# A hybrid decoder layer on one core: when the first q tiles and the scans' step sizes are computed

## What is computed

```python
mod = jax.nn.silu(c) @ w_ada[layer] + b_ada[layer]
sh1, sc1, g1, sh2, sc2, g2 = jnp.split(mod[:, None, :], 6, axis=-1)
h = rmsnorm(x, norm1_g[layer]) * (1.0 + sc1) + sh1
proj = h @ w_in[layer]
q, k, v, ga, gb, z, xbc, dt = jnp.split(proj, offsets, axis=-1)
...
ya = diff_attention(q, k, v, positions, ...)   # rmsnorm and rope of q and k, 8 heads, two softmaxes each
yb = ssd_mixer(z, xbc, dt, ...)
# in ssd_mixer:
dtp = jax.nn.softplus(dt.astype(jnp.float32) + dt_bias.astype(jnp.float32))
a_neg = -jnp.exp(a_log.astype(jnp.float32)).reshape(SSD_GROUPS, SSD_HEADS_PER_GROUP)
y = ssd_chunked(xs * dtp[..., None], dtp * a_neg, bm, cm)   # needs cumulative sums of dtp * a_neg
```

## Time and profile before

| | |
|---|---|
| median of 3 runs | 1936.28 us (1935.77 to 1940.3) |
| profiled execution | 1932.19 us, span 1930.4 us |
| PE busy | 1606.1 us (83%) |
| DVE busy | 1322.3 us (68%) |
| ACT busy | 934.2 us (48%) |
| mean granted clock of PE | 0.915 |

### The profile page before, as it was taken

How to read it: one execution, slowest core, us unless ns; L and a number is a source line. 1 busy time by engine, 2 the same in 40 slices (tenths; PEclk the granted TensorE clock), 3 DMA queues, 4 the chain that set the end, 5 groups by cost and what they waited for, 6 DMA issues and landing times.

```text
span 1930.4 us, 22703 instructions
## 1 busy us (share of the span) xinstructions
PE 1606.1 (83%) x7242; PEld 1255.4 (65%) x7243; DVE 1322.3 (68%) x1714; ACT 934.2 (48%) x1136; POOL 306.1 (16%) x298
## 2 busy tenths in 40 slices
PE   6697698699999999998974728999999779999950
PEld 1485586477777777775863516787777558877740
DVE  2486557777674775766556657798888448888849
ACT  2325433532234343342322127788888448888830
POOL 1000000011020101101100271222222122222210
PEclk9798899899999999998986869999999889999985
DMA  8021022068212122120431049899999459999948
GB/s 287 28 87 44 1 87 88 1 234 313 88 63 88 66 66 88 46 86 3 164 116 66 1 149 353 315 378 376 354 370 385 175 194 371 368 364 357 345 171 355
DMA packets 103538, 361.43 MB, mean 187 GB/s; under 512 B 19116, under 2 KB 29552, under 8 KB 76432
## 3 DMA queue, kind: packets, MB, share of 16 engines
q1 hardware_dynamic: 71472, 278.41, 38.9%
q0 software_dynamic: 27040, 62.07, 8.8%
q10 hardware_dynamic: 4928, 19.78, 2.6%
HBM read 352.18 MB, written 43.66 MB: 205 GB/s over the span
## 4 chain that ended last, share of the span: by engine, by line
PE 60%; DMA 15%; DVE 14%; ACT 4%; issue 4%; POOL 2%; ACTq 0%; SPq 0%; POOLq 0%; DVEq 0%
PE psum L1311 16%; PE psum L1313 15%; PE psum L1312 15%; DMA rawm<-in_w_exp_up 8%; DMA modraw<-in_w_ada 2%; PE psum L720 2%; POOL slot_table L571 2%; DMA rawm<-in_w_exp_down 2%; DVE ring L879 2%; PE psum L1533 2%; DVE ofin L962 1%; PE psum L1478 1%; PE psum L1466 1%; DVE modacc L1632 1%; PE psum L1438 1%
## 5 line engine op out<-in xcount | busy, mean ns | idle before, releaser
L879 DVE TENSOR_TENSOR ring<-rawm,ring 128x2048 fp32r<-128x2048 f32 x192 | 436.0, 2286 | 39.8 <-ACT ring L807 39.6
L807 ACT ACTIVATE ring<-rawm 128x2048 fp32r<-128x2048 f32 x192 | 368.1, 1918 | 94.5 <-DMA rawm<-in_w_exp_up 41.0
L1311 PE MATMUL psum<-ring,xT 128*128 128x512 f32 x528 | 223.8, 424 | 27.2 <-DVE ring L879 22.4
L1618 DVE TENSOR_TENSOR hl<-raw,hl 128x2048 fp32r<-128x2048 f32 x59 | 135.4, 2296 | 119.1 <-ACT hl L1104 118.5
L1313 PE MATMUL psum<-ring,xT 128*128 128x512 f32 x528 | 211.1, 400 | 0.0
L1312 PE MATMUL psum<-ring,xT 128*128 128x512 f32 x528 | 210.9, 399 | 0.0
L1311 PE MATMUL psum<-hl,hT 128*128 128x512 f32 x416 | 165.4, 398 | 11.2 <-DVE hT L1919 11.2
L666 POOL DMA_INDIRECT y_rows<-yb,row_of x64 | 98.4, 1538 | 439.7 <-ACT yb L851 430.1
L1313 PE MATMUL psum<-hl,hT 128*128 128x512 f32 x416 | 162.9, 392 | 0.0
L1312 PE MATMUL psum<-hl,hT 128*128 128x512 f32 x416 | 162.9, 392 | 0.0
L1311 PE MATMUL psum<-hT,hl 128*128 128x512 f32 x320 | 136.9, 428 | 1.3 <-DVE hl L1618 1.3
(11 more groups left out here) (374 smaller groups left out, 3078.7 us busy)
## 6 DMA issues: line engine op xcount, KB each, us to landing
rawm<-in_w_exp_gate SPq DMA_DIRECT2D x64, 1024.0 KB, 11.8
rawm<-in_w_exp_up SPq DMA_DIRECT2D x64, 1024.0 KB, 14.7
rawm<-in_w_exp_down SPq DMA_DIRECT2D x64, 1024.0 KB, 9.6
raw<-in_w_in SPq DMA_DIRECT2D x36, 1024.0 KB, 5.1
modraw<-in_w_ada POOLq DMA_DIRECT2D x16, 1024.0 KB, 7.0
ysum<-y_rows ACTq DMA_DIRECT2D x16, 1024.0 KB, 9.1
raw<-in_w_ada SPq DMA_DIRECT2D x8, 1024.0 KB, 9.7
raw<-in_w_branch_b SPq DMA_DIRECT2D x8, 1024.0 KB, 5.1
```

Of the source, the lines that this page charges most:

```text
L807: A(ring[:, slot, 1, :], rawm[slot][:], ACT.Copy).then_inc(S["m_hi2"], 1)
L879: TT(ring[:, slot, 0, :], rawm[slot][:], ring[:, slot, 1, :].bitcast(F32), ALU.subtract).then_inc(S["m_lo2"], 1)
L1311: M(dst, lhs(0), rhs(0), start=first, stop=False)
L1618: TT(hl[:, slot, 0, :], raw[slot][:], hl[:, slot, 1, :].bitcast(F32), ALU.subtract).then_inc(S["lo_done"], 1)
```

## The change

The first two tiles of q are computed inside the step `h`: two blocks behind the transposes, PE issues the three matmuls of one channel block for each of the two tiles, into banks 0 and 1 (`products`). Their own steps then issue nothing on PE (`ahead`). The step sizes become a step kind of their own, `dt`, in three parts that stand in the list behind q's second tile (the dt weights' products, ACT's copy), behind q's fourth tile (transposes, softplus, `aa`), and behind k's third tile (cumulative sums, exponential, last product). They no longer stand in `h`. This holds for the first four heads; for the others (hf = 1) the list is as it was.

```diff
@@ -87,6 +87,7 @@
 
 
 CONV = (4, 5, 0, 1, 2, 3)
+DT_AT = {("q", 1): 0, ("q", 3): 1, ("k", 2): 2}
 
 
 def plan_steps(w):
@@ -151,8 +152,14 @@
     item("h", 0)
     late = iter([(j, h) for j in range(4, 12) for h in range(2)])
     for hf in range(2):
-        whole(base("row", ("q", hf), halves(w["w_in"], OQ + hf * 512), 4))
-        whole(base("row", ("k", hf), halves(w["w_in"], OK + hf * 512), 4))
+        for n, at in (("q", OQ), ("k", OK)):
+            b = base("row", (n, hf), halves(w["w_in"], at + hf * 512), 4)
+            for o in range(4):
+                out(b, o)
+                if (n, hf) == ("q", 0) and o < 2:
+                    steps[-1]["ahead"] = True
+                if hf == 0 and (n, o) in DT_AT:
+                    item("dt", DT_AT[n, o])
         whole(base("row", ("v", hf), halves(w["w_in"], OV + hf * 512), 4))
         item("qkT", hf)
         item("attn", hf)
@@ -1145,14 +1152,16 @@
                     a.wait_ge(S["params"], 16 * 9)
                     a.wait_ge(S["params_act"], 16 * 7)
                     A(wdt_hl[:, :, 0, :], wdt[:], ACT.Copy).then_inc(S["small_hi"], 1)
+                elif kind == "dt" and tag == 0:
                     a.wait_ge(S["smallT_ps"], 1)
                     A(hsplit[0:32, 0, :], psum[0:32, 6, :], ACT.Copy).then_inc(S["smallT_ev"], 1)
-
+                elif kind == "dt" and tag == 1:
                     a.wait_ge(S["dt_dve"], 1)
                     L(A(dwk[:, 2], dwk[:, 1], ACT.Exp))
                     A(dtb[:, 1], dtb[:, 1], ACT.Exp).then_inc(S["dt_exp"], 1)
                     a.wait_ge(S["dt_dve"], 2)
                     A(dwk[:, 4], dwk[:, 3], ACT.Ln).then_inc(S["dt_exp"], 1)
+                elif kind == "dt":
                     a.wait_ge(S["dt_ps"], 2)
                     A(expo[:].rearrange("p a t h -> p (a t h)"), psum[:, 5, 0:384], ACT.Exp).then_inc(S["dt_exp"], 1)
                 elif kind in ("row", "col", "branch"):
@@ -1313,6 +1322,17 @@
                 return M(dst, lhs(1), rhs(0), start=False, stop=last)
 
 
+            def products(s, k):
+
+                u = s["base"]["u"][k // 4]
+                if s["o"] == 0 and k % 4 == 0:
+                    pe.wait_ge(S["lo_done"], u["m"] + 1)
+                wv = lambda q: hl[:, u["n"] % RING, 1 - q, :].rearrange("p (k n) -> p k n", n=512)
+                ins = three(bank(s["o"]), lambda q: hT[:, k, q, s["o"] * P:(s["o"] + 1) * P],
+                            lambda q: wv(q)[:, k % 4, :], k == 0, k == KD - 1)
+                if k == KD - 1:
+                    ins.then_inc(S["proj_done"], 1)
+
             pe.wait_ge(S["params"], 16 * 9)
             pe.wait_ge(S["consts"], 1)
             tr(psum[:, 6, 0:113], pr1[0:113, :], ident[0:113, 0:113]).then_inc(S["par_T"], 1)
@@ -1346,29 +1366,38 @@
                     wait(pe, S["mod_ev"], tag)
                     M(bank(7), ones[:], modacc[:, tag % 2], start=True, stop=True).then_inc(S["mod_ps"], 1)
                 elif kind == "h":
+                    ahead = [q for q in steps if q.get("ahead")]
                     pe.wait_ge(S["xr_ready"], NT)
-                    for k in range(KD):
-                        wait(pe, S["h_tmp"], k - 1)
-                        for t in range(NT):
-                            ins = tr(psum[:, 4 + k % 2, t * P:(t + 1) * P], x_rows[:, t, k * P:(k + 1) * P], ident[:])
-                        ins.then_inc(S["xT_ps"], 1)
-
+                    for k in range(KD + 2):
+                        if k < KD:
+                            wait(pe, S["h_tmp"], k - 1)
+                            for t in range(NT):
+                                ins = tr(psum[:, 4 + k % 2, t * P:(t + 1) * P], x_rows[:, t, k * P:(k + 1) * P], ident[:])
+                            ins.then_inc(S["xT_ps"], 1)
+                        if k >= 2:
+                            pe.wait_ge(S["h_lo"], k - 1)
+                            for q in ahead:
+                                products(q, k - 2)
+                elif kind == "dt" and tag == 0:
                     pe.wait_ge(S["small_lo"], 1)
-                    pe.wait_ge(S["h_lo"], KD)
                     for k in range(KD):
                         ins = three(psum[0:32, 6, :], lambda q: wdt_hl[:, k, q, :], lambda q: hT[:, k, q, :],
                                     k == 0, k == KD - 1)
                     ins.then_inc(S["smallT_ps"], 1)
+                elif kind == "dt" and tag == 1:
                     pe.wait_ge(S["smallT_ev"], 1)
                     for t in range(NT):
                         ins = tr(psum[:, 4, t * 32:(t + 1) * 32], hsplit[0:32, 0, t * P:(t + 1) * P], ident[0:32, 0:32])
                     ins.then_inc(S["dt_ps"], 1)
+                elif kind == "dt":
                     pe.wait_ge(S["dt_dve"], 3)
                     for q, tri in enumerate((upper, later, ones)):
                         for t in range(NT):
                             ins = M(psum[:, 5, (q * NT + t) * 32:(q * NT + t + 1) * 32], tri[:], aa[:, t, :],
                                     start=True, stop=True)
                     ins.then_inc(S["dt_ps"], 1)
+                elif s.get("ahead"):
+                    continue
                 elif kind in ("row", "col", "branch"):
                     name, b, o = tag[0], s["base"], s["o"]
                     nk = len(b["u"]) * b["ks"]
@@ -1737,6 +1767,7 @@
                     L(TT(dt_, dwk[:, 2], dwk[:, 5], ALU.add))
                     L(TT(aa[:], dtp[:], over_h(dtb[:, 1]), ALU.mult))
                     TS(aa[:], aa[:], -1.0, None, ALU.mult).then_inc(S["dt_dve"], 1)
+                elif kind == "dt" and tag == 2:
                     v.wait_ge(S["dt_exp"], 3)
                     L(TT(dtdec[:], dtp[:], expo[:, 1], ALU.mult))
                 elif name in ("q", "k"):
```

## The result

| | before | changed |
|---|---|---|
| median | 1935.38 us (1927.39 to 1940.3, 8 runs) | 1924.85 us (1919.26 to 1928.27, 8 runs) |
| ratio | | 0.9948, 95% interval 0.9926 to 0.997 |
| profiled execution | 1932.19 us, span 1930.4 | 1925.31 us, span 1923.5 |

The change makes the kernel faster, by 0.5% in this comparison. It repeated at 0.9966 (0.9949 to 0.9983) and 0.9961 (0.9945 to 0.9977) with the same code. The forecast was 0.3%, and 1924.85 us lies under its range of 1926 to 1938.

What follows compares the result with a forecast made beforehand. PE was taken to bound the changed stretch, DVE close behind. PE's earlier q tiles, less the 9.5 us wait and 2.3 us of clock, ended v 5.8 us sooner: 1930.5 us from the 1936.28 median, range 1926 to 1938.

Steps and rivals of the forecast that it cites:

- both q tiles done: End of step h: q's first two tiles, computed among the transposes, finish at 73.8 us; bounds 72 and 84.
- clock behind it: PE's k third tile after the idle time: 4.6 us at half rate, a loss of 2.3 us; bounds nothing and 5.4.
- scan matrices: PE's 24 small matmuls after k's third tile: 3.3 us, between 2.6 and 5.1, where they took 5.14 before.
- shift at v's end: PE's turn from v's last tile to q's transposes: 149.5 in place of 155.3, 5.8 us sooner.
- The hold: Second dt part waits for q's norm on DVE and delays ACT's first k eviction; PE idle 9.5 us before k's third tile.
- the variant with -4.4: A 1.38 us drain per table switch would lengthen the wait for k's eviction by 1.4 us, making the sum -4.4.
- The interleaved part: Rival: the eight rounds among the transposes in h run at low clock; +6.6 us, 1942.9 us, chance 0.08.
- Slow and stay slow: Rival: low clock lasts through k's third tile, scan matrices and seven next products; net +0.2, 1936.5 us, chance 0.17.
- a change without the hold: Rival: ACT evicts k before the second dt part, DVE becomes the bound; -17.7, 1918.6 us, chance 0.05.
- The paragraph ahead of the rivals: Took the shift of 5.8 us to 1926.4 against the profiled execution and 1930.5 against the median of 1936.28 us.
- How the numbers follow: Section giving the forecast 0.70; chances faster 0.48, same 0.41, slower 0.11; range of 1926 to 1938 us.
- the bound: What a measurement of this kernel tells from no change: 0.3%, 5.8 us, just the forecast shift.

Runs made afterwards that it cites:

- the filled hold: Against the changed kernel, 40 products without use on PE ahead of k's third tile; 11.8 us under the kernel before, ratio 0.9939.
- the kernel with ACT's share later: Against the changed kernel, only ACT's share of the second dt part moved, behind k's second eviction; 6.9 us under the kernel before, ratio 0.9964.

## Why the prediction was right and wrong

The path was right, nearly to the microsecond. Counted from the first scaled tile, in the profile of the changed kernel:

| step, as predicted | predicted | measured |
|---|---|---|
| both q tiles done | 73.8 - 56.4 = 17.4 us | 75.48 - 57.93 = 17.55 |
| PE idle at k's third tile | 9.5 us | 9.16 from start to start, 9.00 idle |
| clock behind it | 2.3 us | 8.18 - 5.44 = 2.74 |
| scan matrices | 3.3 us | 2.60 |
| shift at v's end | 5.8 us | 99.08 - 92.93 = 6.15; 6.6 on the means of three |
| the whole, by ratio | 5.8 us | 10.0, 6.6 and 7.5 |

The hold was where it was put, with the engines named: ACT waited 17.11 us for `dwk`, PE for ACT. The Trainium skill (TensorE: Matmul & The Clock Gate, "HAM oscillation — how this bites in real kernels") says that a burst of products behind an idle stretch starts cold. The changed kernel's trace agrees, with a mean of 0.66 over the 8.18 us behind the hold, and the filled hold priced that at 2.6 us apart from the wait. The drain beside a table load, which the prediction takes from the Trainium skill (ScalarE: Activation LUTs, "What ACT_TABLE_LOAD costs"), isn't there: the logarithm began 1.29 us after the load (110.41, 111.70), so the variant with -4.4 falls.

Some of the agreement is luck. In `h` the clock rose about 5.5 us after the first scaled tile, where I had 4.4 (60.8 - 56.4): it stood at 0.50 over 60 to 62 and at a mean of 0.64 over 62 to 64. Rounds of 1.83 us, where I had 1.9, made up for most of that. And I read the earlier trace rows wrongly: DVE's split that starts at 153.55 takes 2.29 us and so ends behind v, not 2 us short of its end. It cost nothing, since in the changed kernel the same split ends at 148.2, ahead of the transposes at 150.66.

**Of the rivals.** The interleaved part didn't run at the low clock: 0.84 over the 17.55 us, with the slow part at its start. Slow and stay slow didn't come about either, as the matrices at 1.00 show; the kernel with ACT's share later shows that it does come about when a wait stands right ahead of them. And a change without the hold, which I had at 1918.6 us and -17.7, is real as another kernel: the second part one tile earlier, -18.5.

**The step that failed** is the time from which the shift was taken. The paragraph ahead of the rivals takes 5.8 us off the median of three executions, 1936.28 us, as if that were fixed, and under "How the numbers follow" the range of 1926 to 1938 is made from the costs of the clock and the rivals alone. The scatter between executions and comparisons was put at nothing without a reason, though the view was there: 1935.77 to 1940.3 us for three runs of one kernel, and the profiled one at 1932.19. What the runs showed in its place: the same kernel before had medians of 1928.47, 1926.68 and 1928.25 us in the three later comparisons, 8 to 10 us lower. From 1928.25 the same shift of 5.8 gives 1922.5, and the changed kernel measured 1921.98 and 1921.39 there. In the first comparison the kernel before did come out at 1935.38, and there the gain itself came out large: 10.0 us with an interval of 5.8 to 14.3, which holds the stage's 6.6. What made up the other 3.4 in that one comparison isn't shown.

A term of 4.1 us for scatter (1936.28 - 1932.19), taken off the low end of the forecast's own range, 1927.5, would have reached 1923.4. The stage's own shift was low by 0.3 us in this profile and 0.8 on the means (scan matrices 0.7 and hold 0.3 shorter than said, the clock 0.4 dearer, the rest in smaller steps), and that alone would not have missed. For the chances, the same: with 5.8 us just on the bound, faster at 0.48 was as open as the sum allowed.

## What to carry to other kernels

Before a step is moved behind another on one engine, list what that engine still has ahead of it and what stands behind it on every other engine that shares the step: one place earlier in the list was worth 12 us here, with the same work. Price a wait of TensorE together with the clock behind it, and read in the rows how long the work behind it stayed at the low level: here a wait of 4.73 us cost another 4.8 that way. Where the expected shift is no larger than the scatter between a kernel and itself, that scatter belongs in the range, and stages are to be compared by their lengths in several profiles.

## What the runs showed of the hardware

Each of these comes from one or a few profiles of this case. The clock stayed down while the small scan matrices (24 records of 128x32) ran, though PE was busy throughout: 5.14 us at 0.50 in the kernel before, 5.4 us at 0.54 behind a wait of 4.73 us. Where it stood at 1.00 when they began, they ran at 1.00, in 2.60 us. With sixty bf16 products of 128 columns in the wait ahead of `h` the clock read 1.00 behind it, where it had read 0.52 without them. And a wait of the same length ahead of the same work (2.64 to 2.67 us) was followed by a fall of the clock in some executions and not in others (0.91 and 1.00 over the same stretch), in both kernels.
